# Key projection of the memory: high and low parts side by side in one 512-column operand

## The reference

```python
def memory_cross_attention(h, m, w_q, w_kv, w_o):
    q = (h @ w_q).reshape(bsz, seq, MEM_HEADS, MEM_HEAD_DIM)
    k, v = jnp.split(m @ w_kv, 2, axis=-1)
    ...
    s = jnp.einsum("bqhd,bkhd->bhqk", q, k, ...) * (MEM_HEAD_DIM ** -0.5)
    p = jax.nn.softmax(s, axis=-1).astype(v.dtype)
    o = jnp.einsum("bhqk,bkhd->bqhd", p, v).reshape(bsz, seq, D_MODEL)
    return o @ w_o
...
def second_block(x, mem, ...):
    for layer in range(DEPTH):
        ...
        x = x + rmsnorm(y, g_mix_post[layer])
        h = rmsnorm(x, g_cross_pre[layer])
        m = rmsnorm(mem, g_mem[layer])
        y = memory_cross_attention(h, m, w_xq[layer], w_xkv[layer], w_xo[layer])
        x = x + rmsnorm(y, g_cross_post[layer])
        ...
```

## Time and profile before

| | us |
|---|---|
| median of 3 runs | 2760.85 |
| lowest, highest | 2757.74, 2761.82 |
| span of the profiled execution | 2758.4 |
| PE busy | 2702.3 (98%) |
| DVE busy | 1018.9 (37%) |
| ACT busy | 1093.4 (40%) |
| POOL busy | 1273.4 (46%) |

### The profile page before, as it was taken

How to read it: one execution, slowest core, us unless ns; L and a number is a source line. 1 busy time by engine, 2 the same in 40 slices (tenths; PEclk the granted TensorE clock), 3 DMA queues, 4 the chain that set the end, 5 groups by cost and what they waited for, 6 DMA issues and landing times.

```text
span 2758.4 us, 37206 instructions
## 1 busy us (share of the span) xinstructions
PE 2702.3 (98%) x13426; PEld 2227.3 (81%) x13426; DVE 1018.9 (37%) x1857; ACT 1093.4 (40%) x1754; POOL 1273.4 (46%) x713
## 2 busy tenths in 40 slices
PE   9999999999999999999999999999999999999997
PEld 7777888888877888888878788888887888888886
DVE  6674322115453222105555225221147643422212
ACT  7664323225564332223255234322237443433221
POOL 3654444444454444444445534444444463444442
PEclk9999999999999999999999999999999999999998
DMA  4301232233302222332313312232322341232231
GB/s 180 115 2 47 97 101 91 99 107 100 103 24 74 98 91 99 102 105 79 107 45 123 116 56 82 91 102 97 106 84 95 104 153 46 69 107 91 99 106 61
DMA packets 69220, 252.06 MB, mean 91 GB/s; under 512 B 7680, under 2 KB 7936, under 8 KB 68864
## 3 DMA queue, kind: packets, MB, share of 16 engines
q1 hardware_dynamic: 68112, 247.43, 26.6%
q10 hardware_dynamic: 1008, 3.28, 0.4%
HBM read 248.58 MB, written 2.10 MB: 91 GB/s over the span
## 4 chain that ended last, share of the span: by engine, by line
PE 89%; DVE 6%; ACT 3%; issue 1%; DMA 0%; POOL 0%; DVEq 0%; SPq 0%; POOLq 0%; ACTq 0%
PE ps L628 25%; PE ps L629 25%; PE ps L630 25%; PE ps L795 3%; PE ps L833 2%; PE ps L818 2%; PE ps L737 1%; PE ps L739 1%; PE ps L738 1%; ACT pr L1229 1%; DVE ps L2017 1%; DVE x L2021 1%; DVE xl L1668 1%; PE ps L1040 1%; PE ps L1041 1%
## 5 line engine op out<-in xcount | busy, mean ns | idle before, releaser
L540 POOL TENSOR_TENSOR w_lo<-w_raw,w_hi 128x1024 fp32r<-128x1024 f32 x460 | 1109.8, 2417 | 1297.2 <-ACT w_hi L1160 1294.5
L628 PE MATMUL ps<-xh,w_hi 128*128 128x512 f32 x2260 | 885.9, 392 | 10.9 <-POOL w_lo L540 4.8
L630 PE MATMUL ps<-xh,w_lo 128*128 128x512 f32 x2260 | 880.6, 390 | 0.0
L629 PE MATMUL ps<-xl,w_hi 128*128 128x512 f32 x2260 | 880.4, 390 | 0.0
L1160 ACT ACTIVATE w_hi<-w_raw 128x1024 fp32r<-128x1024 f32 x462 | 485.0, 1055 | 529.3 <-PE ps L630 475.0
L628 PEld LDWEIGHTS ps<-xh,w_hi 128*128 128x128 f32 x2260 | 425.0, 188 | 107.1 <-issue 11.9
L630 PEld LDWEIGHTS ps<-xh,w_lo 128*128 128x128 f32 x2260 | 424.8, 188 | 88.9
L629 PEld LDWEIGHTS ps<-xl,w_hi 128*128 128x128 f32 x2260 | 425.0, 188 | 87.7 <-issue 1.0
L629 PE MATMUL ps<-hl,w_hi 128*128 128x512 f32 x704 | 273.9, 389 | 0.0
L628 PE MATMUL ps<-hh,w_hi 128*128 128x512 f32 x704 | 273.9, 389 | 0.0
L630 PE MATMUL ps<-hh,w_lo 128*128 128x512 f32 x704 | 273.9, 389 | 0.0
(11 more groups left out here) (299 smaller groups left out, 2971.7 us busy)
## 6 DMA issues: line engine op xcount, KB each, us to landing
w_raw<-weights_in SPq DMA_DIRECT2D x462, 512.0 KB, 3.2
x<-x_in SPq DMA_DIRECT2D x4, 512.0 KB, 7.5
mem<-mem_in ACTq DMA_DIRECT2D x2, 1024.0 KB, 4.8
x_out<-x SPq DMA_DIRECT2D x4, 512.0 KB, 2.6
rope<-rope_in SPq DMA_DIRECT2D x1, 512.0 KB, 10.4
tab<-tables_in ACTq DMA_DIRECT2D x2, 256.0 KB, 2.7
tab<-tables_in SPq DMA_DIRECT2D x1, 384.0 KB, 10.7
small<-small_in ACTq DMA_DIRECT2D x1, 326.5 KB, 4.6
```

What stands on the lines that cost most here:

```text
L540: nc.gpsimd.tensor_tensor(w_lo[:, slot], w_raw[:, slot], w_hi.bitcast(f32)[:, slot], ALU.subtract).then_inc(lo_ready, 1)
L628: nc.tensor.matmul(dst, w_hi[:, slot, w], hi, start=first, stop=False)
L629: nc.tensor.matmul(dst, w_hi[:, slot, w], lo, start=False, stop=False)
L630: return nc.tensor.matmul(dst, w_lo[:, slot, w], hi, start=False, stop=last)
```

## The change

mem_h and mem_l become the two halves of one tile mem_hl, side by side for each k. The key projection multiplies w_hi with both halves at once, 512 columns, into the whole bank: columns 0 to 255 get w_hi·high, 256 to 511 get w_hi·low. w_lo·high is added to the first half. At eviction DVE reads the first half into k_x and the second into a piece of tmpb, each times the inverse norm, and adds them behind `add_normed`; the addition takes the place of the nop. The value chunks keep their three matmuls.

```diff
-        mem_h = place("mem_h", [P, KT, MEM], 32, f32r)
-        mem_l = place("mem_l", [P, KT, MEM], 40, f32r)
+        mem_hl = place("mem_hl", [P, KT, 2, MEM], 32, f32r)
+        mem_h, mem_l = mem_hl[:, :, 0], mem_hl[:, :, 1]
...
+            def product_in_halves(bank, slot, tile, hi, both, first, last):
+
+
+                w = slice(tile * P, (tile + 1) * P)
+                nc.tensor.matmul(bank, w_hi[:, slot, w], both, start=first, stop=False)
+                return nc.tensor.matmul(bank[:, 0:MEM], w_lo[:, slot, w], hi, start=False, stop=last)
...
-                linear(name, KT, lambda m, k: (mem_h[:, k, :], mem_l[:, k, :]), n=MEM,
-                       ready=kv_ready, after_first=sum_squares)
+                linear(name, KT, lambda m, k: (mem_h[:, k], mem_hl[:, k].rearrange("p a n -> p (a n)")),
+                       ready=kv_ready, after_first=sum_squares, multiply=product_in_halves)
...
-                    scaled(k_x[:, m], bank, MEM, rstd_m).then_inc(evac_done, 1)
+                    n1 = mark(scaled(k_x[:, m], bank, MEM, rstd_m))
+                    part = tmpb[:, 1, (m % 2) * MEM:(m % 2 + 1) * MEM]
+                    scaled(part, bank[:, MEM:2 * MEM], MEM, rstd_m).then_inc(evac_done, 1)
                     if m >= 2:
                         publish_from_bank(m - 2, f"cross_pre{e}")
                     add_normed(y_mid, f"mix_post{e}", m)
+                    dve.wait_ge(dve_self, n1)
                     dve.wait_ge(evac_done, BANK0[f"xkv{e}"] + m + 1)
-                    V.engine_nop().then_inc(proj_ready, 1)
+                    V.tensor_tensor(k_x[:, m], k_x[:, m], part, ALU.add).then_inc(proj_ready, 1)
```

More of the change, by code:

```diff
@@ L630, in product, with linear @@
                 return nc.tensor.matmul(dst, w_lo[:, slot, w], hi, start=False, stop=last)
-            def linear(name, n_k, rhs, n=T, ready=None, after_first=None, looped=True, in_fourth=None):
+            def product_in_halves(bank, slot, tile, hi, both, first, last):
+                w = slice(tile * P, (tile + 1) * P)
+                nc.tensor.matmul(bank, w_hi[:, slot, w], both, start=first, stop=False)
+                return nc.tensor.matmul(bank[:, 0:MEM], w_lo[:, slot, w], hi, start=False, stop=last)
+            def linear(name, n_k, rhs, n=T, ready=None, after_first=None, looped=True, in_fourth=None,
+                       multiply=product):
                 c0, g0, tiles = CHUNK0[name], BANK0[name], TILES[name]
@@ L651, in out_tile @@
                         hi, lo = rhs(m, k)
-                        last = product(ps[:, g % 4, 0:n], c % RING, k % CT, hi, lo, k == 0, k == n_k - 1)
+                        last = multiply(ps[:, g % 4, 0:n], c % RING, k % CT, hi, lo, k == 0, k == n_k - 1)
                         if k % CT == CT - 1 or k == n_k - 1:
@@ L2050, in publish_memory @@
                     V.scalar_tensor_tensor(out=mem_l[:, m], in0=mem[:, m], scalar=gain(f"mem{e}", m),
-                                           in1=fp(mem_h)[:, m], op0=ALU.mult,
+                                           in1=mem_h[:, m].bitcast(f32), op0=ALU.mult,
                                            op1=ALU.subtract).then_inc(mem_ready, 1)
```

## The result

| | before | after |
|---|---|---|
| median of 5 runs, us | 2760.85 | 2782.71 |
| lowest, highest | 2757.74, 2761.82 | 2778.37, 2784.50 |
| span of the profiled execution | 2758.4 | 2778.2 |

A forecast was written before the change was run, and what follows sets the result against it. PE bounds the kernel as a whole, but DVE is slower in the key projection. Waits of 2 x 9.8 = 19.6 us plus 1.7 of clock make 21.3; on the median of 2760.85 that gives 2782, range 2769 to 2790.

The forecast's parts named there:

- DVE's time passes through to PE: Key projection: DVE, 3.11 us a tile against PE's 2.88, delays ACT's copies, then w_hi, POOL's w_lo and PE.
- The alternation of free and held additions: Key projection: a held addition pushes the next to the end of the next L540; forecast with alternating holds, chance 0.75.
- the 0.20 us behind L540's end: Key projection: a 256-column addition held by POOL's L540 ends 0.20 us after that L540 does.
- Rival A: Key projection: additions slip by L540 and cost 0.34 us each; PE 5.0 us late a layer, 2771 us; chance 0.15.
- 9.8 us a layer: Value chunk 4 starts at 1527.47 instead of 1517.68, waiting for w_lo; 19.6 us over two layers.
- PE's waits at the value chunks: PE waits for w_lo 3.1 us at value chunk 0, then about 1.0, 2.4, 1.0 and 2.4 us.
- drops ahead of chunk 4: Clock drops before value chunk 4 are covered by the next wait and add nothing.
- The clock: Half clock for 3.3 us behind value chunk 4's wait, counted in one of two layers: 1.7 us; range none to 6.6.
- C: Rival: PE's lead is enough, DVE's lateness ends in buffers, only PE's 1.6 us show; 2759 us; chance 0.03.
- D: Rival: mem_hl's 512-column matmul takes longer than 0.2275 us; it would not move the sum; no chance given.
- the rows' price of 0.0125 us a pair: Key projection on PE: 0.360 us a triple becomes 0.3475 a pair; 1.6 us in both layers if PE were the limit.
- the 2.5 ns: Key projection on PE: worth of each removed matmul by the skill's gap formula N/2.4 + 2.5 ns; 0.3 us in all.

The follow-up runs named there:

- e2: The changed kernel's matmuls, but DVE evicts only the first half, the nop is back and w_hi·low is left out of k; 2759.65 us.
- e4: The changed kernel without the addition: the second bank read stays, the nop is back, k lacks w_hi·low; 2763.40 us.
- e6: The kernel before the change, with ACT's three copies of a tile standing one tile later; 2758.02 us.
- e1: The changed kernel with the second half scaled in place in PSUM, so the addition has one input in SBUF, and the nop back; 2770.34 us.
- e8: The changed kernel's matmuls, second halves kept aside, one 128x2048 addition in the query projection, ACT's copies two tiles later; 2757.95 us.
- e3: The changed kernel without the second bank read; the addition stays and adds what tmpb held before; 2772.56 us.

## Why the prediction was right

- **The place.** The step "DVE's time passes through to PE", by way of ACT's copies, w_hi and w_lo, was right. Three runs show it from three sides: e2 (less work on PE alone brings nothing), e4 (0.34 us a tile more on DVE costs 2.6 us a layer) and e6 (with w_hi one tile earlier PE's waits are gone).
- **The hold.** The alternation of free and held additions came tile by tile as worked out, and the 0.20 us behind L540's end measured 0.21. Rival A, no holding, gave 5.0 us a layer; e1, which is that case, measured 5.7. Its tiles are 3.89 us apart, not 3.79: with the nop back, the next bank read starts 0.45 us behind the start of the addition and not 0.33. Over seven tiles that is the missing 0.7 us.
- **The sum.** 9.8 us a layer was forecast, 9.6 measured in the second layer, where no clock drop lies behind the last wait; 2782 was forecast, 2782.71 measured. PE's waits at the value chunks were foreseen as 3.1, 1.0, 2.4, 1.0, 2.4; the profile has 2.57, none, 1.54, 0.79, 2.05. They read 0.2 to 0.5 us shorter. Part of it is that the profile counts idle time from a matmul's modelled end, 0.16 us after the next could start (0.28 long, 0.12 apart). The second wait and part of the third went into a clock drop behind value chunk 0's wait (0.50 from 1510 to 1513 us), as the prediction said of drops ahead of chunk 4.
- **The clock.** Of the two waits at chunk 4, one in each layer, one was counted as followed by a drop, at 1.65 us, and one was, at 1.56 us (57.63 - 56.07). That it was exactly one in the profiled execution is luck. The prediction also read 0.50 for the stretch of the earlier trace rows, whose row has 0.56 as its mean; by that the loss is 3.3 x 0.44 = 1.45 us.
- **The rivals.** C (PE's lead is enough) fell with the wait at value chunk 0. D (the 512-column matmul of mem_hl takes longer than 0.2275 us) fell too: pairs start 0.35 us apart. That spacing, and e8 against e6, bear out the rows' price of 0.0125 us a pair, and not the 2.5 ns that the prediction works out from the Trainium skill (TensorE: Matmul & The Clock Gate, Back-to-back issue gap). That page gives the formula for an isolated matmul, not for a stream of them.
- **Luck.** That forecast and median agree within 0.7 us is better than the working deserves. The five runs of the changed kernel spread over 6.1 us, the profiled ones differ by 19.8 us where 21.3 was forecast, and 0.9 us of the difference between forecast and measured lies outside the stages.

## What to carry to other kernels

Before taking work from the busiest engine, find out in that stretch which engine sets the pace, and through which instruction, standing behind which wait, its lateness gets to the busiest one. A DVE operation with both inputs in SBUF can't be counted at its own duration while POOL runs long operations that read SBUF: an addition of 0.42 us took up to 2.50 here. Read one input from PSUM, or put the operation where POOL is idle. If the preparation of a later step stands in an engine's program behind a wait for a slower engine, try moving that wait back; by one or two steps it cost nothing here (e6, e8).

## What the runs showed of the hardware

**The hold.** DVE additions with both inputs in SBUF that were issued while POOL's L540 ran went on only behind its end (0.21 us behind it in the two rows above); with one input in PSUM (e1) none of sixteen was held. The operation's width does not decide it: 512 columns waited until L540's end and so did 256. It works both ways: a 128x2048 addition held an L540 for some 1.5 us (3.87 against 2.39).

**The rhythm.** The lateness is not in proportion to the added work. Every second addition from tile 2 on was held, and the engines fell in step with periods of 3.8 and 5.1 us in turn (bank reads of tiles 3 to 7 at 1499.88, 1503.64, 1508.75, 1512.55 and 1517.64).

**The clock.** The length of a PE wait did not by itself say whether the granted clock would halve. In the changed kernel it fell to 0.50 behind the waits of 2.57 and 2.69 us at value chunk 0 and behind the 2.05 at chunk 4 of the first layer, and stayed at 1.00 behind the 2.04 at the same place of the second. In e3 it fell behind waits of 1.88 and 1.93 us and not behind one of 1.94.
